# Staggering the parts of a ring of split weights by 64 bytes in a float32 kernel of two network blocks

## What is computed

```python
# first block
h = modulated_rmsnorm(x, c);  u = h @ w_in              # 1024 x 8080 columns: three mixers and their gates
y = rwkv7_scan(u), depthwise_conv(u), mlstm_scan(u)     # recurrences over 512 + 256 tokens, chunked
x = x + gate * (merge(y, p_a, p_b, p_c) @ w_out)
x = x + gate * (square(relu(h2 @ w_mlp1)) @ w_mlp2)     # 1024 -> 4096 -> 1024
# second block, two layers
h = layer_norm(alpha * h + 0.5 * swiglu(h, ffa_w_in, ffa_w_out))   # 1024 -> 2 x 2816 -> 1024
h = layer_norm(alpha * h + concat(gated_delta_rule, stick_breaking, mla)(h @ mix_w_in) @ mix_w_o)
h = layer_norm(alpha * h + 0.5 * swiglu(h, ffb_w_in, ffb_w_out))
h = h + sigmoid(h @ ple_w_gate) * (p @ ple_w_proj)
```

## Time and profile before

| | before |
|---|---|
| median of three runs | 4,083.42 us |
| lowest and highest run | 4,081.65 and 4,089.67 us |
| the profiled execution | 4,090.37 us |
| its span, first to last instruction | 4,088.6 us |
| TensorE (PE) busy | 3,896.2 us, 95% |
| weight loads (PEld) busy | 3,170.3 us, 78% |
| VectorE (DVE) busy | 2,103.5 us, 51% |
| ScalarE (ACT) busy | 1,309.5 us, 32% |
| mean granted clock of TensorE | 0.97 |

### The profile page before, as it was taken

The page is one execution under the profiler, slowest core; times in us unless marked ns, Lnnn a source line. Parts: engine busy times, 40 slices in busy tenths (PEclk is TensorE's granted clock), DMA queues, the critical chain, the costliest instruction groups (busy, mean ns, idle before and its releaser), DMA issues.

```text
span 4088.6 us, 71017 instructions
## 1 busy us (share of the span) xinstructions
PE 3896.2 (95%) x30810; PEld 3170.3 (78%) x30810; DVE 2103.5 (51%) x2922; ACT 1309.5 (32%) x1891; POOL 144.6 (4%) x193
## 2 busy tenths in 40 slices
PE   8998978999999999999989999999999998999998
PEld 5766768887778888888768688887888767688887
DVE  4977466755444445334755453345333746553335
ACT  4253333213323323222422532223222332532222
POOL 0000012220000000000000000000000000000000
PEclk8999878999999999999999999999999989999999
DMA  6213000023342223333102032322323201123331
GB/s 253 71 63 99 7 2 3 3 72 140 124 134 99 93 97 99 103 93 103 53 3 82 11 109 93 103 98 88 103 93 104 63 12 57 37 88 103 93 103 52
DMA packets 319751, 327.81 MB, mean 80 GB/s; under 512 B 10064, under 2 KB 243552, under 8 KB 318032
## 3 DMA queue, kind: packets, MB, share of 16 engines
q1 hardware_dynamic: 312144, 287.01, 21.9%
q0 software_dynamic: 7296, 36.27, 2.4%
HBM read 314.86 MB, written 8.39 MB: 79 GB/s over the span
## 4 chain that ended last, share of the span: by engine, by line
PE 74%; issue 12%; DVE 9%; ACT 3%; DMA 1%; POOL 0%; DVEq 0%; ACTq 0%; SPq 0%; POOLq 0%
PE psum L247 72%; DVE arena L301 2%; PE psum L254 2%; ACT arena L351 1%; DVE arena L312 1%; DVE ring L301 1%; DVE r L301 1%; DVE ring L332 1%; ACT r L351 1%; ACT ring L351 1%; DVE arena L332 1%; DMA ring<-in_w_ada 0%; DVE ring L308 0%; DVE arena L316 0%; DVE arena L306 0%
## 5 line engine op out<-in xcount | busy, mean ns | idle before, releaser
L247 PE MATMUL psum<-r 128*128 128x512 f32 (+2 forms) x12960 | 2847.6, 381 | 30.6 <-DVE r L301 28.4
L247 PEld LDWEIGHTS psum<-r 128*128 128x128 f32 x12960 | 2343.7, 188 | 521.2 <-DVE r L301 28.5
L301 DVE TENSOR_TENSOR r<-ring,r 128x2048 fp32r<-128x2048 f32 (+2 forms) x261 | 573.7, 2198 | 322.3 <-ACT r L351 318.7
L351 ACT ACTIVATE r<-ring 128x2048 fp32r<-128x2048 f32 (+2 forms) x261 | 478.6, 1834 | 362.9 <-PE psum L247 310.4
L351 ACT ACTIVATE arena<-psum 128x512 f32<-128x512 f32 (+7 forms) x509 | 268.1, 527 | 999.5 <-PE psum L247 923.5
L247 PE MATMUL psum<-arena 64*64 64x64 f32 (+11 forms) x5854 | 486.6, 271 | 35.0 <-DVE arena L301 9.7
L247 PEld LDWEIGHTS psum<-arena 64*64 64x64 f32 (+5 forms) x5854 | 313.9, 155 | 175.9 <-issue 100.4
L301 DVE TENSOR_TENSOR arena<-arena,psum 128x512 f32<-128x512 f32 (+4 forms) x217 | 136.3, 628 | 582.5 <-PE psum L247 563.5
L247 PE MATMUL psum<-ring 64*64 64x64 f32 (+3 forms) x7792 | 302.5, 232 | 44.7 <-DVE ring L332 12.8
L247 PEld LDWEIGHTS psum<-ring 64*64 64x64 f32 (+2 forms) x7792 | 262.0, 142 | 68.8 <-issue 30.8
L351 ACT ACTIVATE r<-arena 128x512 fp32r<-128x512 f32 (+1 forms) x176 | 109.4, 622 | 503.0 <-DVE arena L301 500.8
(11 more groups left out here) (113 smaller groups left out, 1532.3 us busy)
## 6 DMA issues: line engine op xcount, KB each, us to landing
ring<-in_ffa_w_in SPq DMA_DIRECT2D x88, 512.0 KB, 4.7
ring<-in_ffb_w_in SPq DMA_DIRECT2D x88, 512.0 KB, 4.7
ring<-in_w_mlp SPq DMA_DIRECT2D x32, 1024.0 KB, 5.2
ring<-in_w_in SPq DMA_DIRECT2D x31, 1024.0 KB, 5.2
ring<-in_w_ada SPq DMA_DIRECT2D x24, 1024.0 KB, 5.2
ring<-in_mix_w_in SPq DMA_DIRECT2D x24, 1024.0 KB, 5.1
ring<-in_ffa_w_out SPq DMA_DIRECT2D x20, 1024.0 KB, 4.9
ring<-in_ffb_w_out SPq DMA_DIRECT2D x20, 1024.0 KB, 5.0
```

Source lines behind the costliest of these rows:

```text
L247: ins = self.raw.matmul(o, l, r, start=start, stop=stop, skip_group_check=True)
L301: self.done(self.raw and self.raw.tensor_tensor(o, a, b, f), keys)
L351: self.done(self.raw and self.raw.activation(o, i, f, scale=scale, bias=bias), keys)
```

## The change

`STEP` = 16 numbers are 64 bytes. The ring becomes 6 x 16 numbers longer, and its six split parts begin 0, 64, 128, 192, 256 and 320 bytes behind a multiple of 2048, in the order hi 0, lo 0, hi 1, lo 1, hi 2, lo 2. The raw parts stay where they are. `m.mod` and `m.small` are cut ahead of `m.hL` and fill the gap that its rounding leaves, so that `m.hL` lies 2048 bytes further and all that is cut behind it lies where it did; `m.tmp` and `m.cst` lie 384 bytes further. The ends of the two lenders are written as `7 * SLOT`, the same number as before.

```diff
 SLOT = 2048
 NSLOT = 3
 ARENA = 53200 - 472
-RING = 3 * SLOT * NSLOT
+STEP = 16
+RING = 3 * SLOT * NSLOT + 6 * STEP
 HEAD = 480
...
     K.raw = [K.mem[0][:, SLOT * z:SLOT * z + SLOT] for z in range(NSLOT)]
-    parts = K.rounded(SLOT * NSLOT, 2 * SLOT * NSLOT)
-    K.hi = [parts[:, 2 * SLOT * z:2 * SLOT * z + SLOT] for z in range(NSLOT)]
-    K.lo = [parts[:, 2 * SLOT * z + SLOT:2 * SLOT * z + 2 * SLOT] for z in range(NSLOT)]
+    parts = K.rounded(SLOT * NSLOT, 2 * SLOT * NSLOT + 6 * STEP)
+    parts = [parts[:, (SLOT + STEP) * i:(SLOT + STEP) * i + SLOT] for i in range(2 * NSLOT)]
+    K.hi, K.lo = parts[0::2], parts[1::2]
...
+    m.mod = view(al(96), [2, 48], [1, 2])
+    m.small = al(256)
     m.hL = A.operand(8, 512)
     mk_h = A.top - 8192
     m.hflat = view(m.hL, [1, 8192])
     m.silcv = view(m.silc, [2, 8], [1, 2])
-    m.mod = view(al(96), [2, 48], [1, 2])
-    m.small = al(256)
...
-    lend, lend_raw = lender(K, end=RING - 2 * SLOT), lender(K, 0, 2 * SLOT)
+    lend, lend_raw = lender(K, end=7 * SLOT), lender(K, 0, 2 * SLOT)
...
-    lend = lender(K, end=RING - 2 * SLOT)
+    lend = lender(K, end=7 * SLOT)
```

## The result

The changed kernel takes 4,136.97 us (median of 4 runs, 4,131.2 to 4,148.78) against 4,082.53 us for the kernel before (4 runs, 4,079.28 to 4,089.67). The ratio is 1.0135, with a 95% interval from 1.0108 to 1.0162. So it is slower by 54.4 us, where I had forecast no effect, and it lies outside my range. The profiled execution took 4,131.20 us.

What follows compares the result with a forecast made beforehand. TensorE, busy 95% of the span, was taken as bound by the step between wide products, 226.6 ns. All terms were 0, so the forecast stayed at the runs' median, 4,083 us; range 4,058 to 4,112.

Steps and rivals of the forecast that it cites:

- surplus of 13.5 ns: Wide products at 2.4 GHz: step of 226.6 ns against 213, half of the 426 ns step at 1.2 GHz.
- The term for the ring: Effect of the shifted ring parts on the wide products' steps: 0, bounded by 133 us less and 46 us more.
- argument from rates: Weights at 4.6 and moving columns at 9.6 bytes a ns slide past each other, so shifting starts changes nothing.
- Rows 4: Timeline of two stretches of 192 wide products, ring as weights and ring moving: both 43.68 us, step 226.6 ns.
- rival 1: Starting addresses clash in the wide products and staggering helps: 3,950 us for all, 4,061 for one step in six; chance 0.17.
- Rows 7: Products with sixteen weight columns, chunks 64 bytes apart: step 231 ns, 4.7 above 226.6, read as the price of shape.
- 46 us more: Upper bound for the ring's parts: 4.7 ns on each of 9,860 products reading a shifted part.
- Rows 8: Plain float32 products whose moving operand crosses a multiple of 2048: 428 ns per pass, crossing costs at most 1 ns.
- count of 9,860 shifted products: 7/9 of 12,672 products with 128 weight columns, 512 or 256 wide, taken to read a shifted ring part.
- Rival 2: Moving rounded operands crossing a multiple of 2048 pay at the full rate: 4.7 ns on 4,219 products, 4,103 us; chance 0.27.
- larger price: Shifted weight loads paying as well as moving operands: 46 us more, 4,129 us; one in four of the 0.27, 0.07.
- split, load and arena terms: Splits on ScalarE and VectorE, loads to raw slots, and moved scratch and constants: 0 each, the last bounded by +3 us.

Runs made afterwards that it cites:

- m1: Kernel of bare rounded products without the computation, starts of weights and moving operand varied: 226.7 ns at distance 0, 228.9 to 234.3 at other multiples of 32 bytes.
- m3: Bare products, starts alternating between 0 and d: at 64 bytes 231.7 ns with own pair alike, 233.3 with next weights alike; at 256 bytes 226.7 to 227.3.
- e2: Changed kernel with the six ring parts 0, 256, 256, 512, 512 and 512 bytes behind a multiple of 2048: 4,085.65 us, ratio 0.9995 to the kernel before.
- m2: Bare products with finer distances, other column counts and plain float32: 229.9 to 239.2 ns for all but one of 24 pairs of starts; plain float32 429 ns.
- e5: Changed kernel with high parts at multiples of 256 bytes and low parts 64 bytes behind them: 4,130.23 us, ratio 1.0130 to the kernel before.
- e1: Changed kernel with the six ring parts back at multiples of 2048 bytes, the rest of the arena still moved: 4,089.11 us, ratio 0.9998 to the kernel before.

## Why the prediction was wrong

**What bounds the kernel: right.** Its first part said that the step of the wide product decides, that 0.7 ns of it can be measured, and that the surplus of 13.5 ns over half of the slow clock's step is where positions could be at work. The loss is 4.8 ns in that very step and nothing at 1.2 GHz. But it came on top of the surplus; what the 13.5 ns themselves are, the runs do not tell.

**The term for the ring: wrong, in two steps of its working.**
- *"Whatever the starting distance, they meet equally often."* This argument from rates failed. It took the two streams for independent ones at even rates that slide past each other; with no knowledge of how the accesses are arranged it could not say that. The runs show 226.7 ns at equal starts and 233.3 with the weights 64 bytes ahead, with every other engine silent (m1), and the term that I put at 0 measured 4.8 ns on each of the 11,640 wide products, 55.5 us.
- *Rows 4 as evidence.* I reasoned that the activations' slices at 0, 512, 1024 and 1536 bytes would show a dependence on distance if there was one. They are all multiples of 256, and the dependence has a period of 256 bytes (m1, m3, e2). Rows 4 hold one single distance, 0, four times. No wide product of the kernel before shows another, which I wrote down under rival 1 and then gave less weight than it deserved: the trace was silent on the question, and "0, since rows 4 and 7 are nearest" took silence for a measured 0.

*Rows 7* were read rightly, and still misled. Their 4.7 ns are the price of the shape (231.7 at 64 and at 256 bytes in m1). As an upper bound they gave "46 us more", against 55 measured in the wide products, so the bound was too low as well; that the size came near is a coincidence, 4.7 ns of shape beside 4.8 ns of address. *Rows 8* were at half the reading rate, as I noted, and m2 shows that plain float32 has the same 429 ns at all four distances tried: they could not have shown it.

The count of 9,860 shifted products was beside the point. Since a product's neighbours count (e5), and since in slot 0 of the changed kernel those with an unshifted high part take 228.8 and 229.4 ns, the unshifted ones pay too, and the loss spreads over all 11,640.

**The Trainium skill's rule.** The start of the weights against that of the moving operand changes the step by up to 7.6 ns of 226.7 where both are multiples of 32 bytes (m1). The Trainium skill's page "SBUF — State Buffer", section "Who interferes with whom", calls TensorE's two read ports, for the moving operand and for the weights, independent; for rounded float32 at the full clock these runs disagree with what I had drawn from it, a term of exactly 0. It may still be right of the ports: what the reads have in common behind them, or whether the loss arises elsewhere in TensorE, no run here shows. The 215.7 ns of the Trainium skill's page "TensorE: Matmul & The Clock Gate", section "Wait — 56ns, not 53.3ns?", was not reached at any starts tried either, so a clash of starts isn't known to be the cause of the remaining 10.9 ns.

**Rival 1** was right that it is a clash of starting addresses and wrong in its direction: the aligned kernel has the best starts of those tried for the wide products, not the worst. **Rival 2** had the sign and, in its larger price, 4,129 us, nearly the time, but by luck: not the mechanism, and with the price of a shape. Moving operands cross multiples of 2048 in e2 and cost nothing, and its "only the stretches with the ring's parts moving grow" is refuted by the timeline, where both do; that both pay stood only in its larger price. The split, load and arena terms, each 0, were right (the splits' rows, and e1 at 0.9998).

The range followed from the same failed step. It kept 46 us of loss in the sum's bounds, but cut it off by giving it 0.07; 4,136.97 lies 25 us beyond its end of 4,112.

## What to carry to other kernels

Let the weights and the moving operand of rounded float32 products of 128 weight columns and 512 moving ones begin at the same place within 256 bytes, and both at a multiple of 32 bytes, and keep that when something small is cut ahead of them: here the other distances in steps of 32 bytes cost 1 to 3.4% of such a step, its neighbours pay as well, and equal starts of 4, 8 or 16 bytes were slow too (231.1 to 239.2 ns). Before taking a 0 from a row, ask whether the row could have shown anything else: many addresses that are alike in the way that counts are one observation. Where the trace is silent on the very resource that a change touches, a kernel of bare products with the two starts as its only variables settles most of it in one run; here it gave the map of distances, and left open which accesses clash.

## What the runs showed of the hardware that was not expected

- The step of a 512-wide rounded product at 2.4 GHz depends on the two starts, from 226.7 to 239.2 ns (m1, m2), with a period of 256 bytes in their distance, and on the starts of the neighbours; at 1.2 GHz (4.89 us for eleven in before and in the changed kernel) it does not.
- The sign counts: 64 bytes ahead costs the moving operand 2.2 ns and the weights 6.7 (m1).
- At equal starts, products with 32, 64 or 96 weight columns step more slowly than those with 128: 231.7, 230.0 and 230.0 against 226.7 ns (m2).
- For 256 moving columns equal starts are the slower ones, 120 against 118 ns, and for 192 and 128 none of the five pairs of starts tried matters: 111.7 ns (m2).
